# Two of the four weight sums of each block-product pair made by adding transfers issued from GpSimd, with the lower weight row's sign turned

## What is computed

```python
def conv_glu_ffn(a, w_up, conv_w, conv_b, w_down):
    L = a.shape[1]
    up = a @ w_up
    gate, val = up[..., :D_FF], up[..., D_FF:]
    gp = jnp.pad(gate, ((0, 0), (CONV_WIDTH - 1, 0), (0, 0)))
    gc = conv_b
    for j in range(CONV_WIDTH):
        gc = gc + gp[:, j:j + L] * conv_w[j]
    return (jax.nn.silu(gc) * val) @ w_down
```

## Time and profile before

| | |
|---|---|
| median of 3 runs | 2246.25 us |
| profiled execution | 2245.8 us |
| its span | 2244.1 us |
| mean granted TensorE clock | 0.995 of full speed |
| busy: TensorE, VectorE, ScalarE, GpSimd | 2212.5, 1401.2, 842.0, 336.3 us |
| transfers | 260.24 MB, mean 116 GB/s |

### The profile page before, as it was taken

One profiled execution on the slowest core, in us unless ns is written; L12 is line 12 of the kernel. 1 busy time (PEld: TensorE's weight loads), 2 busy tenths in 40 slices (PEclk: granted clock), 3 DMA queues, 4 the chain that ended last, 5 costly groups with the idle time before them and its releaser, 6 DMA issues.

```text
span 2244.1 us, 32719 instructions
## 1 busy us (share of the span) xinstructions
PE 2212.5 (99%) x13132; PEld 1958.9 (87%) x13132; DVE 1401.2 (62%) x1570; ACT 842.0 (38%) x960; POOL 336.3 (15%) x293
## 2 busy tenths in 40 slices
PE   9999999999999999999999999999999999999997
PEld 7887877878888899999999999998888888888886
DVE  7576236553368988888888888886433333346444
ACT  6222236452243444444444444444212122226433
POOL 6992004000000111111111111110000000000001
PEclk9999999999999999999999999999999999999999
DMA  5422221233433333223332233335333332332222
GB/s 216 132 73 94 99 95 64 74 117 131 150 108 108 123 128 126 97 114 126 126 126 100 111 126 126 126 135 218 104 131 114 128 116 90 103 111 96 107 96 75
DMA packets 59081, 260.24 MB, mean 116 GB/s; under 512 B 6320, under 2 KB 15152, under 8 KB 38672
## 3 DMA queue, kind: packets, MB, share of 16 engines
q1 hardware_dynamic: 55504, 247.94, 30.7%
q0 software_dynamic: 3520, 11.54, 1.3%
HBM read 237.43 MB, written 22.02 MB: 116 GB/s over the span
## 4 chain that ended last, share of the span: by engine, by line
PE 88%; POOL 5%; DVE 4%; ACT 1%; issue 1%; DMA 1%; SPq 0%; DVEq 0%; POOLq 0%; ACTq 0%
PE bank L655 28%; PE bank L657 28%; PE bank L656 28%; DMA w_raw<-in_w_in 1%; PE bank L757 1%; DVE w_lo L1883 1%; DVE xs_lo L1504 1%; PE bank L833 0%; DVE Y L1597 0%; POOL QKV L2209 0%; POOL QKV L2189 0%; DVE Y L2085 0%; POOL Y L2225 0%; PE bank L835 0%; POOL QKV L2204 0%
## 5 line engine op out<-in xcount | busy, mean ns | idle before, releaser
L655 PE MATMUL bank<-x_block_hi,w_hi 128*128 128x256 f32 x2240 | 632.1, 282 | 5.0 <-ACT conv_in L1347 1.9
L657 PE MATMUL bank<-x_block_hi,w_lo 128*128 128x256 f32 x2240 | 632.3, 282 | 0.0
L656 PE MATMUL bank<-x_block_lo,w_hi 128*128 128x256 f32 x2240 | 629.6, 281 | 0.0
L1049 ACT ACTIVATE w_hi<-w_raw 128x2048 fp32r<-128x2048 f32 (+1 forms) x134 | 222.5, 1660 | 739.9 <-PE bank L657 739.9
L655 PE MATMUL bank<-xs_hi,w_hi 128*128 128x512 f32 x1152 | 456.3, 396 | 4.8 <-DVE xs_lo L1506 2.6
L657 PE MATMUL bank<-xs_hi,w_lo 128*128 128x512 f32 x1152 | 449.5, 390 | 0.0
L656 PE MATMUL bank<-xs_lo,w_hi 128*128 128x512 f32 x1152 | 449.4, 390 | 0.0
L655 PEld LDWEIGHTS bank<-x_block_hi,w_hi 128*128 128x128 f32 x2240 | 426.3, 190 | 6.3 <-DVE w_lo L1883 3.2
L656 PEld LDWEIGHTS bank<-x_block_lo,w_hi 128*128 128x128 f32 x2240 | 426.5, 190 | 0.0
L657 PEld LDWEIGHTS bank<-x_block_hi,w_lo 128*128 128x128 f32 x2240 | 425.9, 190 | 0.0
L1482 DVE TENSOR_TENSOR w_lo<-w_raw,w_hi 128x2048 fp32r<-128x2048 f32 (+1 forms) x136 | 271.5, 1997 | 109.2 <-ACT w_hi L1049 106.5
(11 more groups left out here) (337 smaller groups left out, 2554.5 us busy)
## 6 DMA issues: line engine op xcount, KB each, us to landing
w_raw<-in_w_up SPq DMA_DIRECT2D x48, 1024.0 KB, 5.2
w_raw<-in_w_down SPq DMA_DIRECT2D x64, 704.0 KB, 4.1
Y<-in_w_up SPq DMA_DIRECT2D x40, 1024.0 KB, 5.9
w_raw<-in_w_in SPq DMA_DIRECT2D x31, 1024.0 KB, 4.8
w_raw<-in_w_out SPq DMA_DIRECT2D x16, 1024.0 KB, 4.9
w_raw<-in_w_pg SPq DMA_DIRECT2D x16, 1024.0 KB, 4.7
mid_kept<-val POOLq DMA_DIRECT2D x44, 256.0 KB, 2.3
mid_raw<-mid_kept SPq DMA_DIRECT2D x15, 512.0 KB, 5.2
```

Of the source, the lines that this page charges most:

```text
L655: nc.tensor.matmul(out, w_h, x_h, start=first, stop=False, skip_group_check=onto)
L656: nc.tensor.matmul(out, w_h, x_l, start=False, stop=False, skip_group_check=onto)
L657: return nc.tensor.matmul(out, w_l, x_h, start=False, stop=last, skip_group_check=onto)
L1049: nc.scalar.activation(w_hi[c % 2][:, 0:width], w_raw[c % 2][:, 0:width], ACT.Copy).then_inc(hi_made, 1)
```

## The change

The lower row of the weights is taken as it is read but with turned sign in the scheme: with A21' = -A21 and A22' = -A22 the sums become S3 = A11 + A21', S2' = A22' + S3 (minus the old S2), S1' = A21' + A22' (minus the old S1) and S4 = A12 + S2'. The value computed from the lower row then comes with the other sign, and x sums and joins turn additions into subtractions where that asks for it.

S3 is now made by a transfer that GpSimd issues and that adds the gate's first half, read from DRAM, onto the value's first half in SBUF (`add_in`). S1 gets a place of its own (`s1_raw`, in `Y[:, 12:16]`): SyncE loads the value's first half into it behind the raw weights of a pair, and GpSimd issues a second adding transfer with the value's second half. Only pair 0 still makes S1 on VectorE (`first_s1`). Before each adding transfer GpSimd waits for the raw weights (or for S1's load) and for the adding transfer of the same kind before it. Since `Y[:, 12:16]` is in use until the end of the last pair's S1, the first eight stored tiles come back in two loads, `Y[:, 8:12]` as before and `Y[:, 12:16]` after the split of S1 of the last pair.

```diff
--- before.py
+++ after.py
@@ -254,6 +254,7 @@
         x_of = {S3: T3, S2: T2, A11: B11, S1: T1, A12: B21, A22: T4, S4: B22}
         y_flat = [Y[:, 4 * r:4 * r + 4, :].rearrange("p k t -> p (k t)") for r in range(2)]
         up_raw = [[w_raw[1][:], w_raw[0][:]], y_flat]
+        s1_raw = [Y[:, 14 - 2 * z:16 - 2 * z, :].rearrange("p k t -> p (k t)") for z in range(2)]
         u2, u3 = u_two[:, 0, :], u_two[:, 1, :]
         mids = [mid_a, mid_b]
         y_back = Y[:, 4:8, :]
@@ -390,6 +391,8 @@
         xb_lo_made = sem("xb_lo_made")
         up_in = [sem(f"up_in{z}") for z in range(2)]
         s3_made = sem("s3_made")
+        s1_in, S1_FROM = y_in[2:4], 16 * PER_BATCH
+        s1_made = sem("s1_made")
         s_made = sem("s_made")
         blk_hi = sem("blk_hi")
         blk_lo = sem("blk_lo")
@@ -405,7 +408,7 @@
         silu_made = sem("silu_made")
         mid_made = sem("mid_made")
         mid_out = sem("mid_out")
-        first_mid_in = [sem(f"first_mid_in{z}") for z in range(2)]
+        first_mid_in, FIRST_MID = [sem("first_mid_in"), y_in[0], y_in[1]], [16, S1_FROM + 16, S1_FROM + 16]
         mid_in = [sem(f"mid_in{z}") for z in range(MID_SLOTS)]
         h_in = [sem(f"h_in{z}") for z in range(3)]
         mid_hi_made = sem("mid_hi_made")
@@ -440,8 +443,12 @@
         def raw_block(c, b):
 
             gate, value = up_raw[c % 2]
-            return {S3: value[:, 0:BLOCK], S2: value[:, 0:BLOCK], A11: gate[:, 0:BLOCK], S1: gate[:, 0:BLOCK],
+            return {S3: value[:, 0:BLOCK], S2: value[:, 0:BLOCK], A11: gate[:, 0:BLOCK], S1: gate[:, 0:BLOCK] if c == 0 else s1_raw[c % 2],
                     A12: gate[:, BLOCK:], A22: value[:, BLOCK:], S4: gate[:, BLOCK:]}[b]
+
+        def sums_made(c, b):
+
+            return {S2: 2 * c + min(c, 1) + 1, S1: 2, S4: 2 * c + 3}[b]
 
         def place(c, b):
 
@@ -581,6 +588,10 @@
                     sp.wait_ge(blk_lo, num(i, FAST_UNROLL * PRODUCTS, PRODUCTS * (c - 1)))
                 for z in range(2):
                     sp.dma_start(up_raw[c % 2][z], src[z]).then_inc(up_in[c % 2], 16)
+                if i is not None or c:
+                    if i is None and c == 1:
+                        sp.wait_ge(xb_lo_made, PRODUCTS)
+                    sp.dma_start(s1_raw[c % 2], src[1][:, 0:BLOCK]).then_inc(s1_in[c % 2], 16)
 
             sp.wait_ge(lo_made, DOWN0)
             up_in_raw(None, 0)
@@ -595,12 +606,14 @@
 
             sp.wait_ge(xb_lo_made, PRODUCTS)
             sp.wait_ge(mid_out, 16 * QT)
-            sp.dma_start(Y[:, HALF_K:KT, :], mid_dram[0:HALF_K].rearrange("t p n -> p t n")).then_inc(first_mid_in[0], 16)
+            sp.dma_start(Y[:, 8:12, :], mid_dram[0:4].rearrange("t p n -> p t n")).then_inc(first_mid_in[0], 16)
             sp.wait_ge(blk_lo, PRODUCTS * (FAST - 1))
             for s in range(2):
                 weights(DOWN0 + s, 0, A["w_down"][s], W_DOWN, free=False)
+            sp.wait_ge(blk_lo, PRODUCTS * (FAST - 1) + S1 + 1)
+            sp.dma_start(Y[:, 12:16, :], mid_dram[4:8].rearrange("t p n -> p t n")).then_inc(first_mid_in[1], 16)
             sp.wait_ge(blk_lo, PRODUCTS * FAST)
-            sp.dma_start(Y[:, 5:HALF_K, :], mid_dram[HALF_K:QT].rearrange("t p n -> p t n")).then_inc(first_mid_in[1], 16)
+            sp.dma_start(Y[:, 5:HALF_K, :], mid_dram[HALF_K:QT].rearrange("t p n -> p t n")).then_inc(first_mid_in[2], 16)
             sp.dma_start(Y[:, 0:5, :], h_dram[:, 0:5, :]).then_inc(h_in[0], 16)
 
             def rest_of_h():
@@ -1306,7 +1319,7 @@
             def mid_half(q, t):
 
                 if q == 0:
-                    act.wait_ge(first_mid_in[t // HALF_K], 16)
+                    act.wait_ge(first_mid_in[t // 4], FIRST_MID[t // 4])
                     act.wait_ge(product_done, PRODUCTS * (FAST - 1) + A11 + 1)
                 else:
                     m = MID_CHUNKS * (q - 1) + t // 2
@@ -1333,9 +1346,11 @@
                 if b in (A11, A12, A22):
                     act.wait_ge(up_in[c % 2], num(i, 32 * (FAST_UNROLL // 2), 32 * (c // 2 + 1)))
                 if b == S3:
-                    act.wait_ge(s3_made, num(i, FAST_UNROLL, c + 1))
-                if b in (S2, S1, S4):
-                    act.wait_ge(s_made, num(i, 3 * FAST_UNROLL, 3 * c + (S2, S1, S4).index(b) + 1))
+                    act.wait_ge(s3_made, num(i, 16 * FAST_UNROLL, 16 * (c + 1)))
+                if b == S1 and c:
+                    act.wait_ge(s1_made, num(i, 16 * FAST_UNROLL, 16 * c))
+                if b in (S2, S4) or b == S1 and c == 0:
+                    act.wait_ge(s_made, num(i, 2 * FAST_UNROLL, sums_made(c, b)))
                 if i is not None or PRODUCTS * c + b >= RING:
                     act.wait_ge(product_done, g - (RING - 1))
                 nc.scalar.activation(ring(w_hi, c, b), raw_block(c, b), ACT.Copy).then_inc(blk_hi, 1)
@@ -1867,9 +1882,9 @@
                 for k in ks:
                     stt(Y[:, k, :], Y[:, k, :], par("ffn", k), rstd[:], ALU.mult, ALU.mult).then_inc(x_normed, 1)
 
-            def x_sum(n, dst, a, b):
-
-                tt(dst, a, b, ALU.subtract).then_inc(x_summed, 1)
+            def x_sum(n, dst, a, b, op=ALU.subtract):
+
+                tt(dst, a, b, op).then_inc(x_summed, 1)
 
             def x_block_rest(b, n):
 
@@ -1885,42 +1900,43 @@
             def sum_s2(i, c):
 
                 dve.wait_ge(blk_lo, num(i, FAST_UNROLL * PRODUCTS, PRODUCTS * c + S3 + 1))
-                tt(raw_block(c, S2), raw_block(c, A22), raw_block(c, S2), ALU.subtract).then_inc(s_made, 1)
-
-            def sum_s1(i, c):
-
-                dve.wait_ge(s_made, num(i, 3 * FAST_UNROLL, 3 * c + 1))
-                dve.wait_ge(blk_lo, num(i, FAST_UNROLL * PRODUCTS, PRODUCTS * c + A11 + 1))
-                tt(raw_block(c, S1), raw_block(c, S2), raw_block(c, S1), ALU.add).then_inc(s_made, 1)
+                tt(raw_block(c, S2), raw_block(c, A22), raw_block(c, S2), ALU.add).then_inc(s_made, 1)
+
+            def first_s1():
+
+                dve.wait_ge(s_made, 1)
+                dve.wait_ge(blk_lo, A11 + 1)
+                tt(raw_block(0, S1), raw_block(0, S2), raw_block(0, S1), ALU.subtract).then_inc(s_made, 1)
 
             def sum_s4(i, c):
 
+                dve.wait_ge(s_made, num(i, 2 * FAST_UNROLL, sums_made(c, S2)))
                 dve.wait_ge(blk_lo, num(i, FAST_UNROLL * PRODUCTS, PRODUCTS * c + A12 + 1))
-                tt(raw_block(c, S4), raw_block(c, S4), raw_block(c, S2), ALU.subtract).then_inc(s_made, 1)
+                tt(raw_block(c, S4), raw_block(c, S4), raw_block(c, S2), ALU.add).then_inc(s_made, 1)
 
             def join_u(i, c):
 
                 dve.wait_ge(m1_kept, num(i, FAST_UNROLL, c + 1))
-                tt(u2, conv_in[:, 2:2 + HALF_T], place(c, S2), ALU.add).then_inc(u2_made, 1)
+                tt(u2, place(c, S2), conv_in[:, 2:2 + HALF_T], ALU.subtract).then_inc(u2_made, 1)
                 dve.wait_ge(u2_made, num(i, FAST_UNROLL, c + 1))
-                tt(u3, u2, place(c, S3), ALU.add).then_inc(u3_made, 1)
+                tt(u3, u2, place(c, S3), ALU.subtract).then_inc(u3_made, 1)
 
             def take_c22(i, c):
 
                 dve.wait_ge(product_done, num(i, FAST_UNROLL * PRODUCTS, PRODUCTS * c + S1 + 1))
                 dve.wait_ge(u3_made, num(i, FAST_UNROLL, c + 1))
                 dve.wait_ge(mid_out, num(i, 16 * FAST_UNROLL, 16 * (c + STD_PAIRS)))
-                tt(val[:, HALF_T:], u3, place(c, S1), ALU.add).then_inc(c22_made, 1)
+                tt(val[:, HALF_T:], u3, place(c, S1), ALU.subtract).then_inc(c22_made, 1)
 
             def take_c21(i, c):
 
                 dve.wait_ge(product_done, num(i, FAST_UNROLL * PRODUCTS, PRODUCTS * c + A22 + 1))
-                tt(val[:, 0:HALF_T], u2, place(c, A22), ALU.add).then_inc(c21_made, 1)
+                tt(val[:, 0:HALF_T], u2, place(c, A22), ALU.subtract).then_inc(c21_made, 1)
 
             def take_c12(i, c):
 
                 dve.wait_ge(product_done, num(i, FAST_UNROLL * PRODUCTS, PRODUCTS * c + S4 + 1))
-                tt(conv_in[:, 2 + HALF_T:], u2, place(c, S4), ALU.add).then_inc(c12_made, 1)
+                tt(conv_in[:, 2 + HALF_T:], place(c, S4), u2, ALU.subtract).then_inc(c12_made, 1)
 
             def convolve(i, c):
 
@@ -1970,7 +1986,6 @@
                 else:
                     block_rest(i, c + 1, S2)
                     block_rest(i, c + 1, A11)
-                    sum_s1(i, c + 1)
                 take_c21(i, c)
 
             std_gate(0)
@@ -1981,16 +1996,16 @@
             x_sum(1, T3, B22, B12)
             std_gate(1)
             dve.wait_ge(x_summed, 1)
-            x_sum(2, T1, B12, B11)
+            x_sum(2, T1, B11, B12)
             x_block_rest(S3, 1)
             std_value(1)
             x_block_rest(A11, 2)
             dve.wait_ge(xb_lo_made, 2)
-            x_sum(3, T2, B22, T1)
+            x_sum(3, T2, B22, T1, ALU.add)
             std_gate(2)
             x_block_rest(S2, 3)
             dve.wait_ge(xb_lo_made, 3)
```

(26 more changed lines are left out.)

## The result

The changed kernel took 2250.83 us, the median of 13 runs (2249.46 to 2253.71), against 2246.25 for the kernel before. Its ratio to before is 1.0022, with a 95% interval of 1.0013 to 1.0030: slower by 0.22%, about 4.6 us. The forecast was 2245.1 us; the measured time lies in its range, but on the side that had a chance of 0.17.

The account below looks back on a forecast made before the run. TensorE, busy 2212.5 of 2244.1 us, bounds the kernel; only 6.28 us in the first two pairs is removable. Steady pairs 0, ends 0, start -1.2 us gave 2245.1 us on the median's scale; eight-in-ten range 2241.0 to 2253.

Parts of the forecast that it names:

- the side that had a chance of 0.17: Whole run: slower than the kernel before by more than 0.2%, covering Rival B and rival C; chance 0.17.
- What bounds the kernel: Block-product stage: TensorE is fully busy in steady pairs; only 6.28 us in the first two pairs can be removed.
- The relief: First two pairs: without GpSimd's sum beside them, S4's sum gives back 2.08 us and the convolution's tap 2.09 us.
- rival D: First two pairs: stretched instructions have another cause than GpSimd's sum, start loses 1.84 us, about 2248 us; chance 0.06.
- S3's transfer in pair 0: Pair 0: adding transfer takes 4.8 us (3.4 to 7), VectorE's queue starts 1.84 us late, pair ends 0.24 us earlier.
- S1 in pair 1: Pair 1: load there at 754.2 us, addition landed at 759.0 to 761.8, pair 2 begins 16.6 us after landing.
- the middle: Start of pair 2: 777.0 us, taken between 775.6 (transfer alone) and 778.4 (bytes doubled), 1.2 us before the old 778.20.
- Doubled: S1's addition in pair 1: its 2.8 us of bytes double beside pair 2's 2 MB of weights, landing at 761.8 us.
- rival C: Pair 1 only: S1's transfer lands after 766 us, pair 2 begins at 782.7, 4.5 us late, 2250.8 us; chance 0.05.
- Rival A: First two pairs: addition is free, transfer lands after 3.2 to 3.4 us, 4.2 to 4.7 us gained, about 2241.6; chance 0.13.
- Rival B: Every pair: store stuck behind slow adding transfers in GpSimd's queue, from 14.4 us for both; 2459 us at 10 each; chance 0.12.
- The ends of the stage: Ends of the stage, including the last pair's late second load of stored products: cost zero.

Follow-up runs that it names:

- the copies: Changed kernel plus two unused 1 MB DRAM-to-DRAM copies behind S1's adding transfer in GpSimd's queue, every pair from pair 1 on; 2293.17 us, ratio 1.0207.
- S1 only: Changed kernel with S3 made by GpSimd's sum in all pairs, S1 still by load and adding transfer; 2250.28 us, ratio 1.0018 to the kernel before.
- both pairs mended: Changed kernel with pair 1's S1 made by VectorE and pair 0's S3 by GpSimd's sum; 2241.04 us, ratio 0.9979 to the kernel before.
- the held weights: Changed kernel with SyncE issuing pair 2's raw weights only after pair 1's S1 has been added; 2255.22 us, ratio 1.0043 to the kernel before.

## Why the prediction was wrong

**What bounds the kernel: right.** TensorE in the steady pairs, 6.28 us in the first two; within the stage, every version without the copies differs from the others there and, but for the 0.19 us of the third pair before, nowhere else that a profile shows.

**The relief: right.** 2.08 and 2.09 us were to come back from S4's sum and from the tap. They took 1.23 and 0.54 us in the changed kernel, and where GpSimd's sum is put back (S1 only) S4's sum takes 3.23 again. So the earlier trace rows's 3.31 and 2.63 were indeed GpSimd's sum: rival D has fallen. With nothing late in front of them the first two pairs are 4.4 us shorter (both pairs mended).

**S3's transfer in pair 0: right in kind, 0.6 us short.** Taken at 4.8 us, range 3.4 to 7; measured 5.4. On the prediction's scale it was issued 0.2 us later than the 721.96 of the sum before. VectorE's queue began at 731.15 - 2.38 = 728.77 instead of the 727.96 forecast, and pair 0 grew by 0.52 us where I had it shrink by 0.24.

**S1 in pair 1: the step that failed.** The prediction had S1's load there at 754.2 us and its addition landed between 759.0 and 761.8, the upper end being the 2.8 us of bytes doubled, and took the middle. On the same scale the load was issued at 751.6, there at 755.9 (4.3 us instead of 3.4), and the addition landed at 765.8, after 9.9 us. Three sizes were off in the same direction: 0.8 us (inherited from S3's transfer in pair 0), 0.9, and for the addition 2.3 to 5.1, which is 3.7 over the middle. They make up 5.4 of the 5.5 us by which pair 2 began later than forecast, and the last is the large one. "Doubled" was no upper bound: it doubled only the 2.8 us of bytes, and it left out the 512 KB for pair 2's S1 in the same stretch; what those 512 KB alone cost isn't shown.

The 2 MB of raw weights suffered in turn: in flight for 13.6 us, from 755.12 until GpSimd could use them at 768.77, where they took 8.7 before (752.2 to the 760.93 of the earlier trace rows). The next step, that pair 2 begins 16.6 us after S1 lands, held to 0.1 us: 768.2 + 16.6 = 784.8, measured 784.88. It is rival C, with the place, the mechanism and the deciding point (766 us, pair 2 at 782.7) that it was given; measured 765.8 and 782.5. What was wrong was its chance of 0.05: it was said to take 15 us from 750.8 on, and 0.8 + 4.3 + 9.9 is 15.0. The figures for the middle came from transfers that flew alone, in a stretch that I knew to be busy. The time lies inside the stated range because that had been drawn wide enough for C.

**Rival A has fallen:** an adding transfer of 512 KB takes 5.1 to 5.4 us alone, and 6.7 in a steady pair behind S3's. **Rival B is a real mechanism,** but not in this kernel: the copies bring it out in the steady pairs, and the held weights, together with the loads beside the store, in pair 1. In a steady pair of the changed kernel the store was issued earlier in the pair than before, 9.7 instead of 11.35 us into the pair, and landed after 2.3 us as before.

**The ends of the stage: right.** From pair 2 to the end of the stage TensorE never waited, the late load of stored tiles included.

**Still open:** the 0.3 to 0.5 us between the 4.30 of the two pairs (4.11 of three) and the 4.6 of the medians; they are below what the runs can tell. That S1's load had to wait for the x blocks is part of the chain, and so is what passes in the 4.4 us before its addition moves a byte: whether GpSimd's queue waits behind the loads' bytes or is set up late isn't shown. Another place for S1's load, free earlier, wasn't tried.

Of the Trainium skill, "DMA: Bandwidth & Descriptors", the section on the anatomy of one DMA gives 2.0 us plus the bytes over 436 GB/s for a transfer that GpSimd issues, an estimate of 3.2 us for 512 KB; the adding transfer took 5.4 alone, so that estimate, which prices no addition, does not hold for it. The same page says, under "Issuing engines are not separate DMA queues", that transfers of all issuing engines run on the same 16 DMA engines; 5.4 us alone against 9.9 in traffic agrees.

## What to carry to other kernels

Work taken from engines that are not the bottleneck is worth only what lies in the few places where the bottleneck waits for them: here two instructions of some 1500, at the start of a stage, and two transfers instead of 79 bought it. In those places everything is late already, so what replaces the work must be priced in the traffic of that very stretch, not by its time alone. And a transfer that is put into a queue moves all that is issued behind it: look for the store that somebody waits for.

## What was not expected of the hardware

TensorE's granted clock fell within the wait in pair 1. The stretches of the changed kernel around it:

```profile
core 0: us, PE busy (x) PEld busy (x) DVE busy (x) ACT busy (x) POOL busy (x), PEclk, DMA share, GB/s
...
768.00:769.00 1.00, 0.00 (x0) 0.00 (x0) 0.00 (x0) 0.68 (x1) 0.23 (x1) 0.96 0.08 33
769.00:770.00 1.00, 0.00 (x0) 0.00 (x0) 0.59 (x1) 1.00 (x2) 0.69 (x2) 0.50 0.00 0
...
771.50:772.50 1.00, 1.00 (x6) 1.00 (x6) 0.83 (x2) 0.00 (x0) 0.00 (x0) 0.50 1.09 213
...
777.00:780.00 3.00, 3.00 (x27) 3.00 (x27) 2.97 (x5) 0.43 (x1) 0.57 (x1) 1.00 0.24 87
```

TensorE had been idle since 766.77. At about 769.0 us, 2.2 us into its wait of 3.91, the clock falls to half, 1.2 of 2.4 GHz, and stays there until about 775.7 us, and S1's product takes 5.20 instead of 2.88 us. The kernel before never waited so long in this stage (1.66 us at most) and kept 1.00. Here it cost nothing at the end of the pair, since the last product waits for VectorE's L1929 anyway, and VectorE waited for no other engine between 769.40 and there:

```profile
781.37 0.41 DVE L1929 TENSOR_TENSOR val<-u_two,bank 128x256 f32<-128x256 f32 x1
```

Where the pair ended with TensorE's own products, it did cost. In the kernel with the held weights the last product of pair 1 took 4.61 us. In the one with the copies, this is the stretch behind a wait of 1.80 us, in a pair of 23.51 us:

```profile
979.00:982.00 3.00, 3.00 (x16) 3.00 (x15) 1.58 (x3) 0.00 (x0) 0.59 (x1) 0.50 0.65 265
```

There the length of the wait doesn't tell alone: the clock fell behind four waits of 1.78 to 1.93 us and not behind those of 2.21 and 2.25.
